# Weight sums of FFN 2 made in the mixing stage of a decoder layer and kept in DRAM

## What is computed

```
x += 1/2 * (silu(h @ w_gate1) * (h @ w_up1)) @ w_down1        # FFN 1, inner width 5504
p  = h @ w_in ; a = latent attention(p) ; r = gated linear recurrence(p)
x += concat(a, r) @ w_out
x += cross attention(h, mem)
x += 1/2 * (silu(h @ w_gate2) * (h @ w_up2)) @ w_down2        # FFN 2, inner width 5504
```

## Time and profile before

| | us |
|---|---|
| median of 3 runs (1886.35 to 1888.1) | 1886.77 |
| profiled execution | 1885.84 |
| its span | 1884.0 |
| TensorE busy | 1877.4 (100%) |
| VectorE busy | 1573.7 (84%) |
| ScalarE busy | 1087.4 (58%) |
| GpSimd busy | 95.4 (5%) |

### The profile page before, as it was taken

How to read it: one execution, slowest core, us unless ns; L and a number is a source line. 1 busy time by engine, 2 the same in 40 slices (tenths; PEclk the granted TensorE clock), 3 DMA queues, 4 the chain that set the end, 5 groups by cost and what they waited for, 6 DMA issues and landing times.

```text
span 1884.0 us, 23266 instructions
## 1 busy us (share of the span) xinstructions
PE 1877.4 (100%) x8824; PEld 1575.1 (84%) x8824; DVE 1573.7 (84%) x2015; ACT 1087.4 (58%) x1473; POOL 95.4 (5%) x98
## 2 busy tenths in 40 slices
PE   9999999999999999999999999999999999999999
PEld 8888888888889888988888888888888888888987
DVE  6999999989999867755676774789999999999986
ACT  7665555555656547545476655656565555555553
POOL 0000000000000001312250000000000000000000
PEclk9999999999999999999999999999999999999999
DMA  9666555666556665555443654455655566655654
GB/s 337 224 196 201 193 198 193 225 201 201 181 187 213 217 224 157 167 179 179 136 156 111 206 192 139 156 181 200 201 184 195 203 205 216 204 195 184 197 192 171
DMA packets 176608, 362.57 MB, mean 192 GB/s; under 512 B 8432, under 2 KB 19696, under 8 KB 175856
## 3 DMA queue, kind: packets, MB, share of 16 engines
q1 hardware_dynamic: 176064, 360.89, 57.4%
q10 hardware_dynamic: 432, 0.19, 0.0%
HBM read 358.95 MB, written 2.10 MB: 192 GB/s over the span
## 4 chain that ended last, share of the span: by engine, by line
PE 87%; DVE 9%; issue 2%; ACT 1%; POOL 1%; DMA 0%; SPq 0%; DVEq 0%; ACTq 0%; POOLq 0%
PE acc L1943 16%; PE acc L1945 16%; PE acc L1944 16%; PE acc L1932 9%; PE acc L1934 8%; PE acc L1933 8%; DVE w_lo L1301 4%; PE small L1945 2%; PE small L1943 2%; PE small L1944 2%; PE small L2144 2%; PE tr L1894 1%; PE tr L1945 1%; PE tr L1943 1%; PE tr L1944 1%
## 5 line engine op out<-in xcount | busy, mean ns | idle before, releaser
L1301 DVE TENSOR_TENSOR w_lo<-w_raw,w_hi 128x1024 fp32r<-128x1024 f32 (+3 forms) x752 | 733.4, 1030 | 52.5 <-ACT w_hi L730 40.5
L730 ACT ACTIVATE w_hi<-w_raw 128x1024 fp32r<-128x1024 f32 (+4 forms) x568 | 507.9, 928 | 149.0 <-PE acc L1945 101.8
L1943 PE MATMUL acc<-w_hi,hT_hi 128*128 128x512 f32 (+1 forms) x920 | 355.0, 386 | 0.0
L1945 PE MATMUL acc<-w_lo,hT_hi 128*128 128x512 f32 (+1 forms) x920 | 353.4, 384 | 0.0
L1944 PE MATMUL acc<-w_hi,hT_lo 128*128 128x512 f32 (+1 forms) x920 | 353.1, 384 | 0.0
L1230 DVE TENSOR_TENSOR w_lo<-w_raw,w_hi 128x1024 fp32r<-128x1024 f32 (+1 forms) x184 | 218.3, 1226 | 59.6 <-ACT w_hi L730 58.2
L835 ACT ACTIVATE w_hi<-w_raw 128x1024 fp32r<-128x1024 f32 (+1 forms) x184 | 190.3, 1044 | 118.1 <-DVE w_raw L1289 72.6
L1943 PE MATMUL acc<-w_hi,actT_hi 128*128 128x512 f32 x528 | 207.1, 392 | 0.3
L1945 PE MATMUL acc<-w_lo,actT_hi 128*128 128x512 f32 x528 | 205.7, 390 | 0.0
L1944 PE MATMUL acc<-w_hi,actT_lo 128*128 128x512 f32 x528 | 205.6, 389 | 0.0
L828 ACT ACTIVATE w_hi<-w_raw 128x512 fp32r<-128x512 f32 (+3 forms) x184 | 149.4, 830 | 90.9 <-PE acc L1945 89.9
(11 more groups left out here) (306 smaller groups left out, 2590.5 us busy)
## 6 DMA issues: line engine op xcount, KB each, us to landing
w_raw<-in_ffn_w_down SPq DMA_DIRECT2D x56, 768.0 KB, 4.6
w_raw<-in_ffn_w_down SPq DMA_DIRECT2D x40, 1024.0 KB, 5.3
w_raw<-in_w_in SPq DMA_DIRECT2D x36, 1024.0 KB, 5.1
w_raw<-in_ffn_w_gate SPq DMA_DIRECT2D x38, 768.0 KB, 4.3
w_raw<-in_ffn_w_up SPq DMA_DIRECT2D x38, 768.0 KB, 4.5
w_raw<-in_ffn_w_gate SPq DMA_DIRECT2D x56, 512.0 KB, 3.9
w_raw<-in_ffn_w_up SPq DMA_DIRECT2D x54, 512.0 KB, 4.8
w_raw<-in_ffn_w_up SPq DMA_DIRECT2D x26, 1024.0 KB, 5.8
```

Source lines behind the costliest of these rows:

```text
L730: nc.scalar.activation(piece(w_hi, c % SPLIT, k0, k1, width), piece(raw, c % RAW, k0, k1, width), ACT.Copy).then_inc(hi_done, 1)
L1301: v.tensor_tensor(piece(w_lo, c % RAW, k0, k1, width), piece(raw, c % RAW, k0, k1, width), piece(w_hi, c % SPLIT, k0, k1, width).bitcast(F ...
L1943: mm(dst, lhs_hi, wh, start=first, stop=False)
L1945: return mm(dst, lhs_hi, wl, start=False, stop=last)
```

## The change

In the mixing stage eleven jobs make the weight sums of eleven units of FFN 2: SP loads four tiles into a place of SBUF that is free at that time (four places: A, C, V, G), VectorE makes the sums in place, SP stores the result in the DRAM tensor `kept_sums`. Each job is tied to a step m of `mixer` (2, 5, 8, 11, 14, 17, 20, 24, 28, 32, 36): its first half stands between w_lo of slot m and `mixer(m)`, its second half behind `mixer(m)`. SP issues a job's loads three slots and its store six slots later in its own order than m.

In FFN 2 seven up blocks (1 to 5 of the first half, 0 and 4 of the second) get four units in the order `upupuup` and plain slots of 3, 3 and 2 tiles. In the first four of them units 2 and 3 are prepared ones, in the other three unit 3 alone: their sums are loaded and not made, and of the raw slot three tiles in place of four are loaded. Blocks 1 to 3 of the second half stay as they were. The down pairs of the first half get four units in place of five (`upupupup`) and plain slots of 4, 4, 4, 4 tiles in place of 3, 3, 3, 3, 2. `H_SUMS` of FFN 2 goes from 3 to 4, `A_SUMS` of its first half from 5 to 4.

```diff
+        H_SUMS, A_SUMS = {1: 3, 2: 4}, {1: (5, 3), 2: (4, 3)}
+        READY = {(0, 1): (2, 3), (0, 2): (2, 3), (0, 3): (2, 3), (0, 4): (2, 3), (0, 5): (3,), (1, 0): (3,), (1, 4): (3,)}
+        JOBS = [(h, b, n) for (h, b), ns in READY.items() for n in ns]
+        JOB_STEPS, JOB_PLACES = [2, 5, 8, 11, 14, 17, 20, 24, 28, 32, 36], list("ACVAVAGGGAA")
+        kept = nc.dram_tensor("kept_sums", [len(JOBS), P, 4 * NW], F32, kind="Internal").ap()
...
-                    DUOS.append(Duo(f, True, h, b, min(4, tiles - 4 * b) * P, "upupup", [0, 2, 4], [(6, 4), (10, 3), (13, 3)]))
+                    ready = READY.get((h, b), ()) if f == 2 else ()
+                    DUOS.append(Duo(f, True, h, b, min(4, tiles - 4 * b) * P,
+                                    *(("upupuup", [0, 2, 4, 6], [(8, 3), (11, 3), (14, 2)], ready) if ready else
+                                      ("upupup", [0, 2, 4], [(6, 4), (10, 3), (13, 3)]))))
                 for j in range(DB // 2):
-                    DUOS.append(Duo(f, False, h, j, NW, *(("upupupupup", [0, 2, 4, 6, 8], [(10, 3), (13, 3), (16, 3), (19, 3), (22, 2)]),
-                                                          ("upupupp", [0, 2, 4], [(6, 4), (10, 3), (13, 3), (16, 3)]))[h]))
+                    DUOS.append(Duo(f, False, h, j, NW, *(("upupupupup", [0, 2, 4, 6, 8], [(10, 3), (13, 3), (16, 3), (19, 3), (22, 2)])
+                                                          if (f, h) == (1, 0) else
+                                                          ("upupupup", [0, 2, 4, 6], [(8, 4), (12, 4), (16, 4), (20, 4)])
+                                                          if h == 0 else
+                                                          ("upupupp", [0, 2, 4], [(6, 4), (10, 3), (13, 3), (16, 3)]))))
...
+                    def load_ready(c, k, n):
+                        j = job_of(d, n)
...
+                        sp.wait_ge(slot_used, 2 * (c - RAW + 1))
...
+                        sp.dma_start(tiles[:, :, 0, 0:d.width], rows_of(wg, k, 2, cols)).then_inc(loaded[c % RAW], 16)
+                        sp.dma_start(tiles[:, 1, 1, 0:d.width], wu[(k + 1) * P:(k + 2) * P, cols]).then_inc(loaded[c % RAW], 16)
+                        sp.wait_ge(slot_used, 2 * (c + 1 - RAW + 1))
...
+                        sp.dma_start(made, kept[j].rearrange("p (k n) -> p k n", k=4)[:, :, 0:d.width]).then_inc(loaded[(c + 1) % RAW], 16)
...
+            def job_weights(j):
...
+                if earlier:
+                    sp.wait_ge(job_kept[place], 16 * earlier)
...
+            def job_store(j):
...
+                sp.wait_ge(job_made, j + 1)
...
+                sp.dma_start(dst, src).then_inc(job_kept[place], 16)
...
             for b, n in enumerate(MIX):
                 for s in range(4):
+                    jobs_around(4 * b + s)
...
+            for place in sorted(job):
+                sp.wait_ge(job_kept[place], 16 * JOB_PLACES.count(place))
             load_duos(2)
...
                         if kind == "u" and n:
-                            combine(d.raws[n], u0 + n, w)
-                            lo_parts(d.raws[n], RAW_PARTS, w, u0 + n)
+                            if n in d.ready:
+                                lo_parts(d.raws[n], RAW_PARTS, w)
+                            else:
+                                combine(d.raws[n], unit_number(m, n), w)
+                                lo_parts(d.raws[n], RAW_PARTS, w, unit_number(m, n))
...
+            def job_first(j):
+
+                b = job_tiles(j)
+                dve.wait_ge(job_in[JOB_PLACES[j]], 32 * (JOB_PLACES[:j].count(JOB_PLACES[j]) + 1))
+                done(v.tensor_tensor(b[:, 0, :], b[:, 1, :], b[:, 0, :], ALU.subtract))
+                done(v.tensor_tensor(b[:, 1, :], b[:, 3, :], b[:, 1, :], ALU.subtract))
+
+            def job_second(j):
+
+                b = job_tiles(j)
+                done.wait()
+                done(v.tensor_tensor(b[:, 3, :], b[:, 3, :], b[:, 0, :], ALU.subtract))
+                done.wait()
+                v.tensor_tensor(b[:, 2, :], b[:, 2, :], b[:, 3, :], ALU.subtract).then_inc(job_made, 1)
...
             for m in range(40):
                 lo(M + m, 0, 4, MIX_WIDTH[MIX[m // 4]])
+                if m in JOB_STEPS:
+                    job_first(JOB_STEPS.index(m))
                 mixer(m)
+                if m in JOB_STEPS:
+                    job_second(JOB_STEPS.index(m))
```

More of the change, by code:

```diff
@@ L249, in layer @@
         k_sq = at("k_sq", A0 + 67.5, [P, TT, ROPE])
+        job = {place: at("job_" + place, A0 + kb, [P, 4 * NW]) for place, kb in (("A", 66.5), ("C", 56), ("V", 36), ("G", 44))}
         o_mla = at("o_mla", A0 + 56, [P, TT, AH * P])
@@ L301, in layer @@
         out_done = sem("out_done")
+        job_in, job_kept = ({place: sem(f"job_{name}_{place}") for place in job} for name in ("in", "kept"))
+        job_made = sem("job_made")
         named = {}
@@ L428, in unit_number, with job_of @@
         def unit_number(m, n):
-            return sum(len(d.raws) for d in DUOS[:m]) + n
+            return sum(len(d.raws) - len(d.ready) for d in DUOS[:m]) + sum(i not in DUOS[m].ready for i in range(n))
+        def job_of(d, n):
+            return JOBS.index((d.half, d.block, n))
         def sums_before(f):
-            return (f - 1) * (H_SUMS + sum(A_SUMS))
+            return (f - 1) * (H_SUMS[1] + sum(A_SUMS[1]))
         def sums_number(m, n):
-            return sums_before(DUOS[m].f) + H_SUMS + sum(A_SUMS[:DUOS[m].half]) + n
+            f = DUOS[m].f
+            return sums_before(f) + H_SUMS[f] + sum(A_SUMS[f][:DUOS[m].half]) + n
         def turns_in(d):
@@ L460, in new_sums @@
             d = DUOS[m]
-            return [d.block - 1] if d.up and 0 < d.block <= A_SUMS[d.half] else []
+            return [d.block - 1] if d.up and 0 < d.block <= A_SUMS[d.f][d.half] else []
         FILL_ORDER = ([0, 1, 2, 4], [3, 5, 6, 7])
@@ L804, in flat_x @@
             def flat_x():
-                for n in range(H_SUMS):
+                for n in range(H_SUMS[2]):
                     act.wait_ge(tr_ready[n % 2], groups["x_o"] + n // 2 + 1)
```

112 lines of the change are left out of this document (79 added, 33 removed).

## The result

The change made the kernel slower: 1900.45 us (median of six runs, 1899.9 to 1902.64) against 1886.38 (six runs, 1886.01 to 1888.1), a ratio of 1.0075 with a 95% interval of 1.0064 to 1.0086. The profiled execution took 1900.38 us for a span of 1898.6 us, 14.54 us more than that of before.

What follows compares the result with a forecast made beforehand. TensorE, busy throughout, bounds the kernel, with VectorE nearly full. Less work (-3.2 us), new waits (+13.65) and lost down-pair waits (-1.0) net +9.4, giving 1896.2 us, range 1888.5 to 1904.

Steps and rivals of the forecast that it cites:

- The work: FFN 2: 4.59 us less TensorE work in up blocks, 1.36 more in first-half down pairs, net 3.23 us less.
- The boundary: Between lengthened FFN 2 blocks: VectorE's chain of 25.18 us, begun 0.83 after the last unit, outlasts TensorE's 23.59.
- The hold: TensorE's wait at each boundary of two lengthened blocks: 2.58 us, between 1.0 and 3.3; four boundaries make 10.3.
- VectorE keeps up: Rival for FFN 2: saved combinations let the parts start early enough, nothing is held, 1882.5 us; chance 0.09.
- The rest of FFN 2: Waits in the second half: 0.4 at block 0 to 1, 0.7, 0.9, and 1.0 before the down pair.
- The mixing stage: Eleven jobs cost VectorE 30 us, but TensorE was to lose 0, with 0 to 4 us as bounds.
- the tightest place: Mixing stage, step 2: after the job's second half of 1.4 us, 0.55 us of w_lo's lead is left.
- the rival with a third place: Rival: stores' receipt, SP's waits or jobs at thin leads add +4 to +10 us, 1900 to 1906; chance 0.14.
- the jobs delay w_lo at the thin leads: Mixing stage: one of three mechanisms in a rival of +4 to +10 us on top, chance 0.14 for all.
- the stores' receipt: Mixing-stage DMAs: slow receipt of stores keeps a place of SBUF taken; in a +4 to +10 us rival, chance 0.14.
- SP in `job_weights`: Mixing stage: SP stands waiting there with w_in's loads behind it; in a +4 to +10 us rival, chance 0.14.
- What would show it: Signs: first-half blocks 2 to 5 near 44.3 us, VectorE idle ahead of the parts, TensorE waiting for w_lo, mixing unchanged.

Runs made afterwards that it cites:

- the fourth experiment: The changed kernel with order upuuupp in place of upupuup in the seven lengthened blocks; 1891.08 us, ratio 1.0024 to the kernel before.
- the second experiment: The changed kernel with the jobs' loads and stores but without VectorE's four operations each; 1896.65 us, ratio 1.0053 to the kernel before.

## Why the prediction was right

It said 1896.2 us, 1888.5 to 1904, slower with 0.80; measured 1900.45. The direction and its mechanism hold, and one term was mis-sized. Of the 4.2 us between, the mixing stage makes 3.9, FFN 2 0.7 and the 0.42 ahead of everything 0.4; 0.9 goes off again, because the profiled run of after lies 0.07 us below its median where that of before lay 0.93.

**The work.** 3.23 us less TensorE work: in the fourth experiment blocks 3 and 4 come to 42.07 and 42.06, and block 1 to 41.77, which is 42.45 - 0.68. Right for an up block; the 1.36 us more in the down pairs are counted and not measured by themselves.

**The boundary.** The chain was put at 25.18 us from the parts to the end of unit 1's w_lo, begun 0.83 behind the unit; measured 25.20 (1407.57 to 1432.77). The parts began 0.83 behind the unit too (1406.74 to 1407.57), 0.63 behind the start of ScalarE's copy, and from the unit's end to unit 1's product it was 26.08 us for 23.59 of work. The hold was put at 2.58; blocks 2 to 5 are held for 2.91, 2.62, 2.61 and 2.84, together 10.98, where the sum had 10.3 + 0.35 = 10.65. The order-only run shows that it is this chain: with three tiles more between its ends 0.3 is left. "VectorE keeps up" was the rival that a whole block's balance spoke for; that balance is right too (39.80 of 42.06), and it is not what decides.

**The rest of FFN 2.** Block 1 is held for 0.40, by the parts, for which I had no term. Second half, block 0: 0.38 against 0.4. Blocks 1 to 3: 0.83 against 0.7. Block 4: 0.96 against 0.9, and the down pair behind it 1.14 against 1.0. The down pairs of the first half: +0.11 against +0.36. Together FFN 2 gave +10.2 where the sum had +9.4.

**The mixing stage** is the step that was off: "I take 0, with 0 to 4 us as bounds"; it is 3.94, the very end of them. The reason given was that VectorE is busy for 208.78 of 320 us and that the tightest place is step 2 with 0.55 us left. Step 2 did hold: no slot up to 13 is late. What I didn't do is to read the busy time slot by slot at each of the eleven steps. Before the change slots 14 and 15 show 4.97 and 4.77 of 5.30 us, in the very view that I used for the stage; a job of 2.7 us there could not be free. (2.7 less 0.33 of room is 2.4, and slots 14 to 16 lost 2.5, but that fit is partly luck: slot 15 had room too, and the job's four operations took 4.7 us.) The lead that I looked for, w_lo's ahead of the slot, wasn't the thin one either: `step_take` (L1565 before) ended 0.7 us ahead of the step matmuls, as the two timelines of before show:

```profile
771.55 1.31 DVE L1565 COPY_PREDICATED AT<-level_mask,small 128x256 f32<-128x256 uint8 x2
```

```profile
773.59 1.67 PE L2144 MATMUL small<-wave 128*128 128x64 f32 x14
```

The lead behind 771.55 + 1.31 = 772.86 was too small for two job operations. (TensorE's row is cut by the end of its window.) And two of the job's four operations lasted 1.77 and 1.57 us, not 0.68. For step 17 it is the lead of `step_take`, 0.24, and w_lo of 4.06 us beside GpSimd; room there was enough. The experiments with the jobs alone (+3.9), without their sums (-3.8) and at other steps (-4.0) settle that it is the jobs' work on VectorE at these steps; the split between room, lead and GpSimd is read from the traces. Of the rival with a third place the mechanism "the jobs delay w_lo at the thin leads" is thus the one that came true in kind, at the low end of its price, through the step matmuls' operands; the stores' receipt and SP in `job_weights` cost nothing, by the second experiment.

**The transfers.** The DMA view of after, median us from issue to landing:

```profile
w_raw<-kept_sums SPq DMA_DIRECT2D x10, 1024.0 KB, 5.8
kept_sums<-job_A SPq DMA_DIRECT2D x4, 1024.0 KB, 6.9
kept_sums<-job_G SPq DMA_DIRECT2D x3, 1024.0 KB, 8.5
```

Kept sums land in 5.8 us, not 5.1, still inside the 8.8 they have. By the Trainium skill ("DMA: Bandwidth & Descriptors", Anatomy of one DMA, which describes DMAs issued by GpSimd; these are SP's) a write to HBM can be long in its receipt. The stores took up to 8.5 us, but no run here separates the receipt from the queue ahead of it, and four slots or more covered them.

**What would show it** came: VectorE idle ahead of the parts (1.73), which began 0.83 behind the unit where later than 1 would have been wrong, and blocks of 44.4 to 44.7 where 44.3 was said. TensorE does wait for w_lo, but the prediction put this between units 0 and 1, and more than half of the wait came earlier, inside unit 0. The sign that didn't come was "mixing should take the 320 us it takes now".
